# Token groups of a diffusion backbone: slabs taken in two blocks of four, one token half after the other

## The reference

```python
mix = concat([fourier_mix(f), window_attention(q, k, v, k_ctx, v_ctx, sink)]) @ w_out     # layer 0
mix = (gb * conv3(gc * xv)) @ w_out                                                        # layer 1
x = x + gt_m * rmsnorm(mix, g[1])
x = x + gt_f * rmsnorm(square(relu(modulate(x, g[2], sh_f, sc_f) @ w1)) @ w2, g[3])
mod = silu(c) @ w_mod[l] + b_mod[l]          # 6 x 2048 columns a layer
```

## Time and profile before

| | before |
|---|---|
| median of 3 runs | 2311.14 us (2305.57 to 2317.07) |
| the profiled execution's own time | 2308.09 us |
| its span, first to last instruction | 2306.3 us |
| TensorE busy with products | 2218.4 us, 96% |
| VectorE busy | 1653.4 us, 72% |
| ScalarE busy | 1000.7 us, 43% |
| share of the 16 DMA engines used by the loads | 75.9% |
| mean granted clock of TensorE | 0.98 of full speed |

### The profile page before, as it was taken

One profiled execution on the slowest core, in us unless ns is written; L12 is line 12 of the kernel. 1 busy time (PEld: TensorE's weight loads), 2 busy tenths in 40 slices (PEclk: granted clock), 3 DMA queues, 4 the chain that ended last, 5 costly groups with the idle time before them and its releaser, 6 DMA issues.

```text
span 2306.3 us, 31071 instructions
## 1 busy us (share of the span) xinstructions
PE 2218.4 (96%) x11455; PEld 1821.6 (79%) x11455; DVE 1653.4 (72%) x1773; ACT 1000.7 (43%) x1227; POOL 112.2 (5%) x34
## 2 busy tenths in 40 slices
PE   7898999989999999999979999998999999999998
PEld 3477557778888888888868888887888888888886
DVE  0265734988888878878988889999887654654655
ACT  2173543544344334434444444454443443443443
POOL 0000000100110110110110101101011000000000
PEclk8899999999999999999989999999999999999999
DMA  9966976868888879889867888895887656656664
GB/s 375 361 215 209 376 254 209 298 201 277 288 268 295 288 261 307 283 267 323 301 204 255 284 291 282 284 314 192 285 286 249 203 193 188 190 193 192 200 196 140
DMA packets 253896, 592.63 MB, mean 257 GB/s; under 512 B 18082, under 2 KB 18610, under 8 KB 253234
## 3 DMA queue, kind: packets, MB, share of 16 engines
q1 hardware_dynamic: 253746, 590.63, 75.9%
HBM read 588.46 MB, written 2.10 MB: 256 GB/s over the span
## 4 chain that ended last, share of the span: by engine, by line
PE 87%; DMA 5%; DVE 5%; issue 2%; ACT 1%; SPq 0%; DVEq 0%; ACTq 0%
PE ps L497 30%; PE ps L498 15%; PE ps L560 11%; PE ps L562 11%; PE ps L561 11%; DMA early<-in_w_mod_dram 2%; PE ps L455 2%; PE ps L524 2%; DMA mraw<-in_w_mod_dram 1%; DVE acc L1165 1%; DVE wlo L1155 1%; DMA raw<-in_mlp_w_dram 1%; PE ps L652 1%; DVE junk L1497 1%; ACT whi L830 1%
## 5 line engine op out<-in xcount | busy, mean ns | idle before, releaser
L1155 DVE TENSOR_TENSOR wlo<-raw,whi 128x1024 fp32r<-128x1024 f32 x712 | 897.1, 1264 | 440.0 <-ACT whi L830 438.7
L830 ACT ACTIVATE whi<-raw 128x1024 fp32r<-128x1024 f32 x712 | 751.7, 1059 | 945.4 <-PE ps L498 380.2
L497 PE MATMUL ps<-u,whi 128*128 128x512 f32 x2944 | 1036.2, 397 | 6.6 <-DVE wlo L1155 3.9
L498 PE MATMUL ps<-u,wlo 128*128 128x256 f32 x2944 | 824.6, 280 | 0.0
L497 PEld LDWEIGHTS ps<-u,whi 128*128 128x128 f32 x2944 | 553.2, 188 | 143.3 <-issue 8.7
L498 PEld LDWEIGHTS ps<-u,wlo 128*128 128x128 f32 x2944 | 556.7, 189 | 0.2
L560 PE MATMUL ps<-whi,h 128*128 128x512 f32 x1216 | 475.4, 391 | 8.6 <-DVE wlo L1155 8.6
L561 PE MATMUL ps<-wlo,h 128*128 128x512 f32 x1216 | 474.2, 390 | 0.0
L562 PE MATMUL ps<-whi,h 128*128 128x512 f32 x1216 | 474.1, 390 | 0.0
L1165 DVE SCALAR_TENSOR_TENSOR acc<-mraw,cs,acc 128x1024 f32<-128x1024 f32 x240 | 311.2, 1297 | 3.8 <-DMA mraw<-in_w_mod_dram 3.8
L560 PEld LDWEIGHTS ps<-whi,h 128*128 128x128 f32 x1216 | 228.9, 188 | 58.6 <-DVE wlo L1155 10.9
(11 more groups left out here) (184 smaller groups left out, 1228.2 us busy)
## 6 DMA issues: line engine op xcount, KB each, us to landing
raw<-in_mlp_w_dram SPq DMA_DIRECT2D x512, 512.0 KB, 4.6
mraw<-in_w_mod_dram SPq DMA_DIRECT2D x272, 512.0 KB, 5.3
early<-in_w_mod_dram SPq DMA_DIRECT2D x96, 512.0 KB, 7.2
raw<-in_conv_w_in_dram SPq DMA_DIRECT2D x96, 512.0 KB, 5.3
raw<-in_att_w_in_dram SPq DMA_DIRECT2D x40, 512.0 KB, 4.8
raw<-in_att_w_out_dram SPq DMA_DIRECT2D x32, 512.0 KB, 6.3
raw<-in_conv_w_out_dram SPq DMA_DIRECT2D x32, 512.0 KB, 5.8
raw<-in_w_mod_dram SPq DMA_DIRECT2D x16, 512.0 KB, 7.1
```

What stands on the lines that cost most here:

```text
L497: pe.matmul(bank, whi[:, s % SLOTS, cols], src[:, k, :], start=(k == 0), stop=False)
L498: last = pe.matmul(bank[:, 0:T], wlo[:, s % SLOTS, cols], src[:, k, 0:T], start=False, stop=(k == KC - 1))
L830: act.activation(whi[:, s, :], raw[:, s, :], ACT.Copy).then_inc(hi_ready, 1)
L1155: dve.tensor_tensor(wlo[:, s, :], raw[:, s, :], whi[:, s, :], ALU.subtract).then_inc(lo_ready, 1)
```

## The change

`token_group` is called as before, for the same slabs. Its loops are put differently: the eight slabs are taken in two blocks of four (`SLOTS`). In a block TensorE first makes the products of token half 0 for all four slabs, waiting for each slab ahead of its first use, and then those of half 1 for all four, releasing each slab behind its last. The argument `closing` has no effect any more: before, it made slabs 6 and 7 of a closing group go half by half. Nothing else is touched: loads, `hi`, `lo`, units and rows stand in the same order on their engines.

```diff
-                for s in range(SL - 2 if closing else SL):
-                    slab_waits_all(s)
+                for s0 in range(0, SL, SLOTS):
                     for a in range(2):
-                        last = products(s, a)
-                        if s == SL - 1 and a == 0:
-                            last.then_inc(half_done, 1)
-                    last.then_inc(slab_used, 1)
-                if closing:
-                    slab_waits_all(SL - 2)
-                    products(SL - 2, 0)
-                    slab_waits_all(SL - 1)
-                    products(SL - 1, 0).then_inc(half_done, 1)
-                    products(SL - 2, 1).then_inc(slab_used, 1)
-                    products(SL - 1, 1).then_inc(slab_used, 1)
+                        for s in range(s0, s0 + SLOTS):
+                            if a == 0:
+                                slab_waits_all(s)
+                            last = products(s, a)
+                            if a == 1:
+                                last.then_inc(slab_used, 1)
+                            elif s == SL - 1:
+                                last.then_inc(half_done, 1)
```

## The result

| | before | after |
|---|---|---|
| median of 4 runs each, us | 2312.78 (2305.57 to 2317.07) | 2429.36 (2426.54 to 2431.97) |
| ratio | 1 | 1.0504, 95% interval 1.0482 to 1.0525 |
| the profiled execution's own time, its span | 2308.09, 2306.3 | 2431.97, 2430.2 |

The account below looks back on a forecast made before the run. TensorE, busy 96%, was taken to set the end, VectorE following closely. Terms of 24 + 3 + 56 + 9 + 8 + 7 + 8 - 15 = +100 us on 2308.1 gave 2408 us, range 2366 to 2458.

Parts of the forecast that it names:

- lead of 3h instead of 6h: Token groups, h being 1.36 us for 6 products: next block's first `hi` runs at most 4.08 us ahead of its start.
- Terms 1: Token group behind token group with four unit slabs, 12 in the two MLPs: 2.0 us late each, 24 us.
- 2: First token groups behind another kind, with units, six of them: block 2 is 0.5 us late, 3 us in all.
- 4: GpSimd sums falling into first token groups: 2.9 us late three times, about 0.2 in the other three, 9 us.
- Terms 3: Last three groups of the out stage, conv-out stage and first MLP: units, `finish`, gate rows and sums, 56 us.
- Term 5: Half clock behind the three long waits in the last stages' third groups: 2.6 us lost each, 8 us.
- The unknown half clock: Half clock behind waits of 2.7 to 3.6 us: none taken; at most 10 fall, 16 us.
- The rival that many short stands bring the clock down: About 48 blocks with a wait; 45 costing 1.6 us each add 72 us, giving 2480 us; chance 0.08.
- Term 6: Closing groups release slabs 4 and 5 later, delaying boundaries: 2.9 us at two, 1.6 at the first MLP's, 7 us.
- The rival of the loads: Loads become the bound: half of `hi`'s 101.7 us of load waits come through, 2458 us; chance 0.12.
- no change: Token groups: VectorE's order gives way enough, 96 products take 21.8 us as before, 2308 us; chance 0.04.
- faster: Sums fall in half 1, where TensorE holds four finished slabs, so old waits go: 2293 us; chance 0.03.

Follow-up runs that it names:

- Experiments 1: Kernel after, with VectorE's unit slab instruction working on 8 columns instead of 1024, all loads and waits kept: 2348.7 us.
- 9: Kernel after, with only the unit slabs of the MLPs' token groups moved behind `lo(3)` and `lo(7)`, closing quarter excepted: 2408.7 us.
- 5: Kernel after, with blocks of two slabs instead of four: 2318.0 us, ratio to the kernel before 1.0028.
- 7: Kernel after, with unit slabs, `finish`, `take_row` and gate rows moved behind `lo(3)` and `lo(7)`, unit loads likewise: 2393.4 us, ratio to the kernel before 1.0350.
- 8: Kernel before, with unit slabs, `finish`, `take_row` and gate rows moved behind `lo(3)` and `lo(7)`: 2392.1 us, ratio to the unmoved kernel before 1.0352.
- experiment 3: Kernel after, with slab 3's load put ahead of the third unit slab's load in SyncE's queue, in groups with six unit slabs: 2415.3 us.
- experiment 6: Kernel after, with the four closing groups in the product order of before: 2398.2 us.
- experiment 2: Kernel after, with a unit slab's load bringing 64 columns instead of 1024 from the third unit on, VectorE's instruction kept full: 2415.0 us.
- experiment 4: Kernel after, with GpSimd's sum over the partitions replaced by a `memset` to zero: 2404.6 us.
- experiment 10: Kernel after, with only the last stages' `finish` moved behind `lo(3)` and both gate rows behind `lo(7)`: 2391.4 us.

## Why the prediction was right, and where its sizes were off

The sign, the mechanism and the range held. That the total lies in the range is in part luck: above the forecast my own range had room for half clock and for the second MLP (16 and 12 us), and half of the miss in the last stages, piece (a) below, is neither. Point by point, against the prediction's own steps:

- **What bounds the kernel and the lead of 3h instead of 6h** held. The first `lo` of a run stood 2.73 us ahead of the block, 2.72 was forecast, in every steady group. Experiments 1 and 9 show the mechanism from two sides (work made tiny, work moved), 5 and the pair 7 and 8 show that the order of products costs next to nothing by itself. Four slabs in hand and blocks of four are what makes it dear: at a block's start nothing is released for the next until 5h later.
- **Terms 1, 2 and 4** were right: 35.1 us in the ordinary stages, where they and their restarts gave 35.6; the sum on GpSimd 2.6 where 2.9 stood. A steady group lasts 24.0 us, where 23.8 was forecast. Waits of TensorE were forecast as 90 us in some 80 pieces, and were 83.6 in 81. (The product's 0.2267 us does not follow from 222 products in 50 us, as the prediction has it: that gives 0.2252. It is right all the same, as the groups' 21.76 us for 96 products show.)
- **Terms 3 and 5, the last stages, were mis-sized: 74.1 us against 54.3 with what else falls there.** (The last three groups of the out stage took 27.9, 29.6 and 38.3 us, where 27, 27 and 32 were forecast.) Five pieces make up the 20 us. (a) Block 1 of the three closing groups, "without `finish`, 0.5", was 3.1, 3.7 and 4.3 late, together 9.6 more; 3.0, 3.3 and 3.8 of it are the wait for the fourth slab. I counted five unit slabs where the third entry of `UNIT_EARLY` has six, and I left SyncE's queue out, in which a slab's load stands behind a unit's load that waits for a buffer; experiment 3 gives 2.2 of each back on average, and leaves the 1.2 of three units in the run. (b) Half clock behind two of these waits, 4.5 us. (c) Half clock behind three of the waits of 2.2 us in the groups ahead of them, 4.9 us. (d) Block 2 of the closing groups was 7.9, 8.8 and 8.3 late where 7.4, 7.8 and 7.4 were forecast, 2.4 us. (e) Term 5, the half clock behind the three longest waits, was 2.2, 2.7 and 1.4 us instead of 2.6 each, 1.5 less. (Waits here are read from the distance between products, 0.17 us more than the idle time that a timeline shows; a restart's 0.1 us is left out.)
- **The unknown half clock** was bounded with "at most 10 of them fall, 16 us", and I took none. Five fell, for 9.4 us, (b) and (c). The rival that many short stands bring the clock down was thus partly right, at an eighth of its 72 us; the profile after has a clock of 0.97, and none fell in the first MLP's ordinary quarters.
- **Term 6, the boundaries**, was 5.6 against 7.4, and experiment 6 shows that it is the closing order's. The first MLP's 1.6 was right; the other two were 2.1 and 1.9 instead of 2.9.
- **The rival of the loads** fell by experiment 2, and by the 86.0 us that `hi` waits for them. Its sign, a fourth `hi` that waits for its load and TensorE with it, did show in the three closing groups; but with small unit loads the wait there only fell to about 2 us, and with SyncE's order alone to 1.2 (experiments 2 and 3): the load went out late, and the DMA engines were not the bound. The rival "no change" fell by the waits, and "faster" by the sums, which held a row in block 2 just as the terms had it.
- **The second MLP's later quarters** cost 0.1 us or less each, so the cover of 0.3 us was enough.
- **The rule on who interferes with whom** in the Trainium skill's "SBUF — State Buffer" would have made a held instruction 1.7 us longer. The trace after shows again 4.91 us for a row that takes 0.7 alone, beside a sum recorded with 6.48 us; experiment 4 puts the sums' whole price in quarters 1 and 2 at 2.6 each. The trace agrees with a block, but not over the whole recorded instruction: it ends 1.7 us ahead of the sum's recorded end (below).
- **Not in the prediction at all:** 8.8 us in groups of the other kind, in the first profile. 7.4 of them are a pace that changes from execution to execution (below): 5.1 in the convolution, 0.9, 1.2 and 1.7 in three other stretches, less 1.5 in one that had the slower pace only before. For the other 1.4 us I name no cause. How much of this is in the difference of the medians, 116.6, the executions without a profile do not show.

The miss of experiments 7 and 8 has the same root as (a): I moved work on VectorE and did not follow its loads through SyncE's queue and its two buffers, nor ask what stands behind the last product of a stage. Still open is how much of the boundaries' 30 us there is due to the third unit's load, the sum or the rows behind it; no kernel took these apart.

## What to carry to other kernels

When a loop is put into blocks, compare the block with the number of buffers: with as many slabs in a block as there are buffers, the lead at which a buffer comes free is halved, and an engine that is idle a third of the time becomes the one waited for, because its other work stands in the run where the lead is short. Blocks of half the buffers cost 0.3% here, blocks of all of them 5%. Before other work is moved, follow its loads too: in an in-order queue a load that waits for its buffer holds every load behind it, and that cost TensorE about 2.2 us in each closing group of the kernel after (experiment 3); in experiments 7 and 10 VectorE stood idle for 2.4 and 2.5 us behind such a load.

## What the runs showed of the hardware

**The half clock behind a wait of about 2 us is not a fixed thing.** The same wait of the same kernel was followed by full clock in one profile and by half clock in the other (1.86 us, above). In the first profile (waits by the distance between products, in which the one of 1.86 us counts 2.04) it came behind four of eight waits of 2.2 us, behind none of three of 2.0 to 2.1, behind those of 3.0 and 3.8 us and not behind the one of 3.3. Behind waits of 5.4 us and more it came every time, in both profiles. Behind the shorter ones it costs 1.5 to 3.0 us; behind the fourth of those of 2.2 us, in the first MLP's closing group, the next wait hides it.

**VectorE is held until 1.7 us ahead of the end of GpSimd's sum as the profile records it, whether its turn comes early or late in the sum.** A `gate_row` that is due 0.54 us into a sum of 6.48 us lasts 4.91 us instead of 0.69 (471.82, above). The `lo` of experiment 10 is due 2.41 us into a sum of 6.11 (461.45 against 459.04) and lasts only 3.21 instead of 1.22. Both begin their own work 1.7 us before the sum's recorded end: 471.28 + 6.48 - (471.82 + 4.91 - 0.69) = 1.72, and 459.04 + 6.11 - (461.45 + 3.21 - 1.22) = 1.71.

**The groups of the other kind have two paces.** A pair of products of lines 497 and 498 takes either 0.347 or 0.353 us on average, mostly over a whole stage, at a granted clock of 1.00. Two windows of 50 us in the convolution, in the kernel after, its first profile and its second (columns as the earlier trace rows):

```profile
1350.00:1400.00 50.00, 50.00 (x285) 43.39 (x284) 42.26 (x40) 22.38 (x24) 1.12 (x1) 1.00 0.83 281
```

```profile
1350.00:1400.00 50.00, 50.00 (x291) 44.06 (x289) 43.28 (x39) 22.18 (x24) 3.30 (x1) 1.00 0.86 297
```

285 products against 291. Over the convolution that is 5 us, and no wait stands in it; which stage has which pace differs between executions of one kernel. I have no cause for it. Differences of 5 to 7 us between two profiles should not be read as the work of an edit without a look at this pace.
